# Expert rows by a one-hot product on the tensor engine instead of by table and indirect gather, with three smaller moves, in a two-layer decoder kernel

## The reference, cut to what matters

```
x  += RWKV7(RMSNorm(x));  x += MoE0(RMSNorm(x))
kv  = RMSNorm(x) @ kv_w, compression MLPs
x  += NSA(RMSNorm(x), kv, rel_bias);  x += MoE1(RMSNorm(x));  out = RMSNorm(x)

MoE: group = argmax(xf @ w_gr + b)          (4 groups)
     the 2 best of the group's 8 experts, weights by softmax
     y[t] = sum over its 2 experts e:  weight * (silu(xf[t] @ w1[e]) * (xf[t] @ w3[e])) @ w2[e]
```

## Time and profile before

| | |
|---|---|
| median of 3 runs | 2521.4 us (2521.04 to 2523.46) |
| the profiled execution's own time | 2524.04 us |
| its span | 2521.7 us |
| busy over the span | PE 82%, DVE 29%, ACT 19%, POOL 15% |
| chain that ended last, by engine | PE 60%; DMA 30%; DVE 5%; issue 3%; ACT 2%; POOL 1% |
| of it, the line DMA arena<-m_w (expert weights) | 26% |
| stages (us from the start) | start and projections 0 to 284; bonus loop to 320; scan to 708; w_o to 792; MoE 0 to 1429; NSA to 1886; MoE 1 and the end to 2522 |

### The profile page before, as it was taken

The page is one execution under the profiler, slowest core; times in us unless marked ns, Lnnn a source line. Parts: engine busy times, 40 slices in busy tenths (PEclk is TensorE's granted clock), DMA queues, the critical chain, the costliest instruction groups (busy, mean ns, idle before and its releaser), DMA issues.

```text
span 2521.7 us, 27879 instructions
## 1 busy us (share of the span) xinstructions
PE 2076.5 (82%) x10398; PEld 1168.3 (46%) x10398; DVE 723.1 (29%) x1800; ACT 484.5 (19%) x1207; POOL 372.4 (15%) x650
## 2 busy tenths in 40 slices
PE   8999799999988488778778299988884988877882
PEld 5344289999944233323222147755533333333330
DVE  4204855555574210000000330455403100000002
ACT  2212244444421000000000101255400000000001
POOL 0000366666500100000000100011101000000001
PEclk9999799999998598988899599999995989889996
DMA  9622000000016499999998621100023999999994
GB/s 269 87 75 67 8 2 2 2 2 2 2 51 255 135 400 402 403 402 394 398 403 334 240 67 34 67 26 18 10 100 139 373 401 403 408 405 401 407 417 154
DMA packets 59720, 514.69 MB, mean 204 GB/s; under 512 B 8548, under 2 KB 13412, under 8 KB 42694
## 3 DMA queue, kind: packets, MB, share of 16 engines
q1 hardware_dynamic: 41414, 470.94, 48.7%
q0 software_dynamic: 7936, 25.18, 2.9%
q10 hardware_dynamic: 10240, 16.79, 1.9%
HBM read 475.17 MB, written 36.66 MB: 203 GB/s over the span
## 4 chain that ended last, share of the span: by engine, by line
PE 60%; DMA 30%; DVE 5%; issue 3%; ACT 2%; POOL 1%; SPq 0%; ACTq 0%; DVEq 0%; POOLq 0%; PEldq 0%
PE bank L1269 55%; DMA arena<-m_w 26%; PE bank L1734 2%; DMA arena<-x_rows,ints 1%; DMA arena<-y_rows,ints 1%; PE bank L1279 1%; PE bank L1466 1%; ACT arena L567 1%; POOL token_table L508 1%; DVE arena L1084 0%; DMA y_rows<-arena 0%; PE bank L1541 0%; PE bank L1527 0%; DVE arena L1220 0%; DVE arena L890 0%
## 5 line engine op out<-in xcount | busy, mean ns | idle before, releaser
L1269 PE MATMUL bank<-arena 128*64 128x512 f32 (+10 forms) x8274 | 1805.2, 476 | 213.2 <-DMA arena<-m_w 145.6
L1269 PEld LDWEIGHTS bank<-arena 128*128 128x128 f32 (+3 forms) x8274 | 934.8, 175 | 951.7 <-issue 856.7
L664 ACT ACTIVATE arena<-bank 128x256 f32<-128x256 f32 (+3 forms) x512 | 176.6, 351 | 218.7 <-PE bank L1269 160.8
L692 ACT ACTIVATE arena<-bank 128x512 f32<-128x512 f32 x64 | 38.2, 597 | 900.0 <-PE bank L1269 900.0
L1084 DVE COPY arena<-bank 128x256 f32<-128x256 f32 x64 | 27.1, 424 | 591.0 <-PE bank L1541 591.0
L517 POOL DMA_INDIRECT arena<-x_rows,ints x64 | 57.2, 895 | 880.7 <-PE bank L1527 872.0
L446 POOL TENSOR_TENSOR arena<-arena,const 128x128 f32<-128x128 f32 x384 | 164.6, 458 | 105.2 <-PE bank L1269 83.7
L1068 DVE TENSOR_TENSOR arena<-bank,vec 128x512 f32<-128x512 f32 x64 | 44.3, 692 | 348.2 <-PE bank L1527 348.2
L1527 PE MATMUL bank<-const,arena 64*128 64x64 f32 x512 | 70.3, 280 | 64.8 <-DMA arena<-x_rows,ints 64.8
L1527 PEld LDWEIGHTS bank<-const,arena 64*128 64x128 f32 x512 | 61.3, 200 | 114.2 <-DMA arena<-x_rows,ints 67.2
L788 ACT ACTIVATE arena<-arena,small 128x128 f32<-128x128 f32 (+3 forms) x128 | 70.6, 553 | 96.8 <-DVE small L1220 96.8
(11 more groups left out here) (197 smaller groups left out, 1185.1 us busy)
## 6 DMA issues: line engine op xcount, KB each, us to landing
arena<-m_w SPq DMA_DIRECT2D x64, 4096.0 KB, 36.9
arena<-m_w SPq DMA_DIRECT2D x64, 2048.0 KB, 27.3
y_rows<-arena ACTq DMA_DIRECT2D x128, 128.0 KB, 12.8
y_rows<-arena SPq DMA_DIRECT2D x2, 3840.0 KB, 39.8
arena<-kv_w SPq DMA_DIRECT2D x3, 2048.0 KB, 13.6
rev_bias<-arena SPq DMA_DIRECT2D x1, 5120.0 KB, 69.1
arena<-a_wk SPq DMA_DIRECT2D x8, 512.0 KB, 16.5
arena<-a_wv SPq DMA_DIRECT2D x8, 512.0 KB, 3.5
```

What stands on the lines that cost most here:

```text
L664: nc.scalar.activation(dst(n), src, ACT.Copy).then_inc(sem("ev_" + name), 1)
L1269: return nc.tensor.matmul(dst, lhsT, rhs, start=start, stop=stop)
```

## The change

In the MoE, the normed x, the token table, the index arithmetic for it and the row gathers are gone. DVE makes, for a pair of experts (2p, 2p + 1), a matrix `onehot` of 512 tokens by 128 slots from the place of each token, times the token's 1/rms. PE multiplies columns of `h` with it, which gives the transposed rows of both experts at once: 8 feature blocks of 4 products (128 x 128 with 128 columns), in two halves q. DVE evacuates each half with the gain. `xgT` holds two pairs. The part of the slot arithmetic that serves the results is kept, behind the first pair's work on DVE.

SP's `moe_loads` loses the store of x, the table and the waits for the gathers; the wait of `w_q` moves to `combined` 8 (the end of MoE 0). The bias tables leave the start: their loads are issued after the projections' weights, their 55 products run in groups of 7 in the bonus loop, and ACT evacuates them after it. In NSA, ACT's copy stands ahead of the exponentials in each tick. The path for experts with over 64 tokens is rewritten in the same way and is not shown; no instruction of it is in the trace.

```diff
@@ SP
-            sp.dma_start(fwd, ...); sp.dma_start(rel[0:32, :], ...); sp.dma_start(rev, ...)
             sp.dma_start(h, d["x"]...)
...
-            (the stores of zeros to y_rows, y_clear)
                     if q == 4:
-                        sp.wait_ge(sem("rev_ev"), 1)
-                        sp.dma_start(cmp_dram, bias_made).then_inc(sem("cmp_bias"), 16)
-                        sp.dma_start(rev_dram, spread(rev_rows, 1, P)).then_inc(sem("rev_out"), 16)
+                        sp.wait_ge(sem("zero_rows"), 1)
+                        (the stores of zeros to y_rows, y_clear)
...
+            sp.wait_ge(sem("mix_ready"), 48)
+            (loads of fwd, rel, rev)
+            sp.wait_ge(sem("rev_ev"), 1)
+            sp.dma_start(cmp_dram, bias_made).then_inc(sem("cmp_bias"), 16)
+            sp.dma_start(rev_dram, spread(rev_rows, 1, P)).then_inc(sem("rev_out"), 16)
...
@@ moe_loads
-                    if e == 1:
-                        for j in range(NJ):
-                            sp.wait_ge(sem("xn_ready"), 4 * (1 + 2 * l) + j + 1)
-                            sp.dma_start(x_rows[l][P * j:P * j + P, :], xn_m[:, j, :]).then_inc(sem("x_rows_out"), 16)
-                    if e == 2:
-                        sp.wait_ge(sem("table_out"), 128 * (l + 1))
-                        sp.dma_start(rows_i, table[l]...).then_inc(sem("rows_in"), 16)
-                        sp.wait_ge(sem("gather0"), 16 * (E // 2 * l + 1))
-                        sp.wait_ge(sem("gather1"), 16 * (E // 2 * l + 1))
...
-            sp.wait_ge(sem("hidden_mm"), E)
+            sp.wait_ge(sem("combined"), 8)
             sp.dma_start(w_q, ...)
@@ moe_pool: the 8 table writes and the 32 gathers per layer are removed
@@ ACT, after the loop of operands_act
+            act.wait_ge(sem("bias_mm"), 1)
+            (the four copies L582 to L585, the last with rev_ev)
...
+                        if name == "y" and n == 0:
+                            act.wait_ge(sem("cmp_bias"), 16)
@@ ACT, NSA tick: the block of pT_act (n = tick - 2) stands before the block of Exp (n = tick)
@@ moe_dve, after two_hot
+                dve.wait_ge(sem("place_mm"), at("place_mm", l + 1))
+                then(nc.vector.scalar_tensor_tensor(posm, bank[1][:, 0:128]..., 1.0, two_hot, ALU.add, ALU.mult))
+
+                def one_hot(p):
+                    at_p = onehot[:, p % 2, :, :]
+                    if p >= 2:
+                        dve.wait_ge(sem("gathered_T"), E * l + 2 * p - 2)
+                    then(nc.vector.tensor_tensor(at_p..., spread(spread(cst("iota1"), 1, 2), 1, NJ),
+                                                 spread(posm[:, :, 2 * p:2 * p + 2], 3, CAP), ALU.is_equal))
+                    nc.vector.tensor_tensor(at_p, at_p, spread(rstd, 2, P), ALU.mult).then_inc(sem("onehot_ready"), 1)
+
+                def x_out(p, q):
+                    dve.wait_ge(sem("gathered_T"), E * l + 2 * p + q + 1)
+                    if q == 0 and p >= 2:
+                        dve.wait_ge(sem("hidden_mm"), E * l + 2 * p - 2)
+                    nc.vector.tensor_tensor(xgT[:, p % 2, 4 * q:4 * q + 4, :], bank[2 + q]..., gain, ALU.mult
+                                            ).then_inc(sem("xgT_ready"), 1)
+
+                one_hot(0); x_out(0, 0); x_out(0, 1); one_hot(1)
+                (then the weights of the results, position, count and the slot arithmetic)
...
                     (gated of expert e)
+                    if e % 2 == 0 and e < E - 2:
+                        x_out(e // 2 + 1, 0); x_out(e // 2 + 1, 1)
                     (hT of expert e)
+                    if e % 2 == 1 and e < E - 4:
+                        one_hot(e // 2 + 2)
@@ PE
-            (55 bias products and 2 wide ones, bias_mm, before the first transposes)
...
             for m in range(NP):
                 pe.wait_ge(sem("rk_ready"), m + 1)
-                mm(bank[m][:, :], head_ones, tmp[:, 3, m % 2, :]).then_inc(sem("bonus_mm"), 1)
+                if m >= 4:
+                    pe.wait_ge(sem("bonus_ev"), m - 3)
+                mm(bank[m % 4][:, :], head_ones, tmp[:, 3, m % 2, :]).then_inc(sem("bonus_mm"), 1)
+                if m == 0:
+                    (waits for proj_ev 24, bias_in 48, rel_mask)
+                for at_m in range(7 * m, min(7 * m + 7, NOFF)):
+                    mm(bank[4 + at_m // 32][...], fwd[:, 864 - 16 * at_m:992 - 16 * at_m], rel)
+            mm(bank[6][0:NH, :], rel, rev[:, 0:512])
+            mm(bank[7][0:NH, 0:128], rel, rev[:, 512:640]).then_inc(sem("bias_mm"), 1)
+            pe.wait_ge(sem("rev_ev"), 1)
@@ moe_pe
-                def transpose_rows(n): (8 transposes of xg)
+                def gather(p, q):
+                    pe.wait_ge(sem("onehot_ready"), E // 2 * l + p + 1)
+                    if l or p:
+                        pe.wait_ge(sem("xgT_ready"), E * l + 2 * p + q - 1)
+                    for k in range(4):
+                        for j in range(NJ):
+                            last = mm(bank[2 + q][:, P * k:P * k + P], h[:, j, 4 * q + k::NK], onehot[:, p % 2, j, :],
+                                      j == 0, j == NJ - 1)
+                    last.then_inc(sem("gathered_T"), 1)
...
-                transpose_rows(E * l); transpose_rows(E * l + 1)
+                gather(0, 0); gather(0, 1)
                 first_half(E * l)
                 for e in range(E):
-                    if e < E - 2:
-                        transpose_rows(n + 2)
+                    if e % 2 == 0 and e < E - 2:
+                        gather(e // 2 + 1, 0)
                     if e < E - 1:
                         first_half(n + 1)
+                    if e % 2 == 0 and e < E - 2:
+                        gather(e // 2 + 1, 1)
                     (transpose_gated, result of n)
```

More of the change, by code:

```diff
@@ L231, in decoder_program @@
         row_in, block_of, is_over, slot_f = (scratch(NJ * 2) for _ in range(4))
-        over_cmp = region(2)[:, 0:32 * OVER].rearrange("p (b e) -> p b e", b=OVER)
-        over_expert = region(2)[:, 512:528]
+        posm = scratch(NJ, 32)
+        over_rel = scratch(NJ, 2)
+        over_cmp = region(2)[:, 512:512 + 32 * OVER].rearrange("p (b e) -> p b e", b=OVER)
+        over_expert = region(2)[:, 992:1008]
         over_ids, over_count = ints[:, 120:136], ints[0:1, 136:137]
-        over_rows_i = ints[0:CAP, 137:138]
         combine_w = small[:, 88:96].rearrange("p (j c) -> p j c", c=2)
         slot_i = ints[:, 0:8].rearrange("p (j c) -> p j c", c=2)
[L238 to L242, removed]
         y_rows = [nc.dram_tensor(f"y_rows{l}", (SLOTS, D), FP32, kind="Internal").ap() for l in range(2)]
-        table = [nc.dram_tensor(f"token_table{l}", (SLOTS, 1), I32, kind="Internal").ap() for l in range(2)]
         xT_kv = region(2).rearrange("p (k t) -> p k t", k=NK)
@@ L317, in _ @@
                     if q == 4:
-                        sp.wait_ge(sem("rev_ev"), 1)
-                        sp.dma_start(cmp_dram, bias_made).then_inc(sem("cmp_bias"), 16)
-                        sp.dma_start(rev_dram, spread(rev_rows, 1, P)).then_inc(sem("rev_out"), 16)
+                        sp.wait_ge(sem("zero_rows"), 1)
+                        for l in range(2):
+                            sp.dma_start(y_rows[l][E * CAP:SLOTS, :].rearrange("(p q) c -> p q c", p=OVER * 8),
+                                         spread(zero_rows[0:OVER * 8, :], 1, CAP // 8)).then_inc(sem("y_clear"), 16)
                     if q >= 4:
@@ L780, in _ @@
             for tick in range(len(UNITS) + 4):
+                n = tick - 2
+                if 0 <= n < len(UNITS):
+                    m, b, j = UNITS[n]
+                    act.wait_ge(sem("probs_mm"), at("probs_mm", 2 * n + 2))
+                    if n >= 2:
+                        act.wait_ge(sem("O_mm"), at("O_mm", n - 1))
+                    nc.scalar.activation(probs_T[:, n % 2, 1, 0:P * (j + 1)], bank[5][:, 0:P * (j + 1)],
+                                         ACT.Copy).then_inc(sem("pT_act"), 1)
                 n = tick
@@ L1040, in moe_dve @@
                 then(nc.vector.tensor_copy(over_ids[:, 0:OVER], over_expert[:, 0:OVER]))
-                then(nc.vector.tensor_copy(ints[:, 136:137], over_upto[:, 31:32]))
                 for c, hot in enumerate((hot1, hot2)):
@@ L1273, in norm_transpose @@
                 for k in range(NK):
-                    if i == 0 and k == 4:
-                        pe.wait_ge(sem("rev_ev"), 1)
                     for j in range(NJ):
@@ L1520, in moe_pe, with hidden @@
                 last.then_inc(sem("place_mm"), 1)
-                def transpose_rows(n):
-                    pe.wait_ge(sem(f"gather{n % 2}"), 16 * (n // 2 + 1))
-                    if n >= 2:
-                        pe.wait_ge(sem("xgT_ready"), n - 1)
-                    for k in range(NK):
-                        last = nc.tensor.transpose(bank[2 + n % 2][:, CAP * k:CAP * k + CAP], xg[:, n % 2, k::NK],
```

(14 more changed lines are left out.)

164 lines of the change are left out of this document (66 added, 98 removed).

## The result

The changed kernel takes 2633.4 us (median of 4 runs, 2629.61 to 2635.05), the kernel before 2521.2 beside it (4 runs): ratio 1.0445, 95% interval [1.0429, 1.0462]. It is 112 us slower; the forecast was 107 us faster. The profiled execution has a span of 2633.1 us.

A forecast was written before the change was run, and what follows sets the result against it. It took DMA time, mostly weights, to bound the expert loop, and PE with its waits NSA's loop. Terms -3 - 78 - 8 - 18 = -107 from 2524.0 gave 2417, as a median 2415 us; range 2385 to 2452.

The forecast's parts named there:

- MoE, before the stream: Between the places' end and the first hidden product: 64 new gather instructions at 0.12 to 0.21 us each, 12 us.
- Rival (a): Expert loops: PE takes over as bound, at a mixed 16.9 us per expert, 31 us more, 2445; chance 0.14.
- (e): Expert loops: gathers hold PE at 1.2 GHz, above 3200; slower than before from 18.3 us per expert; chance 0.02.
- t0: Predicted start of MoE 0's first hidden product, 850 us (846 to 854), with 29 expert loads still to go.
- The stream's own rate: Expert loops: without the indirect gathers' 4.5%, weights take 16.44 and 16.28 us per expert; both layers together -78 us.
- (d): All goes well: high clock in bonus loop, 16.0 us per expert, NSA at PE's own time; 2388; chance 0.12.
- (b): Expert loops: the gathers were free to the stream, 17.1 us per expert stay, 44 us more, 2457; chance 0.07.
- Start and bonus loop: Moving the bias work: start gains 14 us, seven loop iterations cost 7 and the end 4; net -3.
- The scan: Scan stage: the new bias table writes to DRAM run there while its DMA is idle, costed at nothing.
- MoE 0's end: Result gathers after MoE 0: with w_q's load behind combined, the first is 7.3 us shorter; -8 us in all.
- NSA: NSA loop: ACT's copy ahead of the exponentials gives -13 us and a higher clock 5 us; -18 in all.
- The gap: Start of each layer's weight stream: DMA idles 9.4 us because expert 3's w2 waits for expert 0's result products.

The follow-up runs named there:

- e5_contig: The changed kernel with features dealt to blocks as 128 neighbours, so that gather products and the transposes before the router read contiguous columns: 2367.7 us, ratio 0.9396 to the kernel before.

## Why the prediction was wrong

**The step that failed** is the price of the gather instruction ("MoE, before the stream"): "None like them is in the trace. Below: 0.11 each, the router's rate at the high clock; above: 1.09 / 8 = 0.136 for a strided load of PE's stationary side". The gather takes 0.244 us an instruction. The upper bound was no bound. L1527 does load 128 columns at a step of 8 floats, and so does `norm_transpose` of the earlier trace rows with all 128 rows; both are transposes, which take 0.11 us from start to start at the high clock with the step or without it (the 0.136 is that plus the end of the last of the eight). What did not carry over is the kind of instruction: from a transpose to a float32 product. The right reading of the rows was that none shows a product with a step, and a price of double was open. Its 32 instructions per expert cost 4 us more than I took, PE's 15.5 us per expert became 19.4, and PE passed the weights' 16.4.

**What it made of the time.** Rival (a), PE takes over the loop, had the mechanism, and I gave it 0.14 with a price of 31 us. It came at the high clock and not the low one, and past (e)'s point of 18.3 us per expert. From the first hidden product (863.4, 13 us later than t0, 10 of them the scan's) to PE's last result (1472.8) MoE 0 takes 609 us. The prediction has 9.4 + 28.67 x 16.44, and as before 22.8 from the last weights to the last result: 503.5. That is 106 us, and 3.6 in the first gathers (15.55 for 12); twice that, for two layers, is 219 of the 222.6 us by which the two MoE stages missed. A PE-bound loop also pays for all 32 experts, where the stream had three in store.

**The stream's own rate** was mis-sized on the other side: 16.4 us per expert, measured 15.4 without gathers. I took the queue's share of engine time for its price. Had the gather instruction cost 0.12 us as I thought, the time would have been about 2368 (run e5_contig), below my range: two errors of opposite sign. The sentence in (d), "if the store and gather neighbours slowed the weights", was right for the gathers. Two sums of the rivals are off by 2 us, without effect on the range: (b) is 2415 + 44 = 2459 and (d) 2415 - 37 = 2378.

**Start and bonus loop**: the terms held. The k-projection's first result came 12.7 us earlier (14 predicted), the loop took 5.10 us per iteration and +7.6 (+7), the end +4.2 (+4). The clock was as the earlier trace rows said. In the window of the bonus loop after,

```profile
274.00:323.00 49.00, 45.55 (x142) 31.08 (x142) 30.99 (x45) 10.18 (x25) 29.58 (x23) 0.50 0.06 14
```

PE is 93% busy and the clock is 0.50 on average. The Trainium skill (TensorE: Matmul & The Clock Gate, Part 1: The HAM clock gate) says that activity releases the throttle; here it did not.

**The scan**: "The new writes of the bias tables to DRAM run in the scan, whose DMA is idle", costed at nothing. I asked who shares the data queue and not who else could be held up. +11.

**MoE 0's end**: the result gather takes 5.64 us against 12.73, and the stretch from the last result to the norm is 6.6 shorter (8 predicted).

```profile
1486.85 5.64 DMA arena<-y_rows,ints
```

**NSA**: right in sign, mis-sized: -18 predicted, -33 in the loop. PE's idle time fell from 28 to 12 us, 16 and not 13, and the clock rose from 0.92 to 1.00, so that its busy time fell from 159 to 142, 17 us where I took 5. At 0.92 PE loses 8% of 187 us, 15: the term was in the earlier trace rows, and I gave back a third of it. The order of ACT's copy does this alone: in the kernel with only that change the same window's clock is 1.00 and PE works 141 of 154 us.

**The gap** of 9.4 us at the stream's start is not in the time: swapping the queue's order changed nothing. In a loop that PE binds the stream makes it up.

## What to carry to other kernels

Before PE reads an operand with a step, find a row with that step in the same kind of instruction: here the transposes with the step were cheap and the float32 products were not. Without such a row, price the product at contiguous and at double, and lay data out so that the columns are neighbours. When a change puts work on the engine that is second in line, work out how near it comes (here 15.5 against 16.4) and ask what one mis-sized term would do: that sets the chance of the rival. A queue's share of the DMA engines need not be all that it costs its neighbours (here 0.77 against 1.8 us per expert). And a long store into a stretch whose DMA is idle was not free.

## What the runs showed of the hardware

- Float32 products of 128 x 128 with 128 columns, per instruction at the high clock: 0.12 us with steps of 1 and 2 floats between the columns of the stationary operand, 0.24 with 4 and 8, and 0.24 with step 8 on the moving side; with 64 moving columns and step 8 still 0.24. The strided product took 0.240 us at a granted clock of 0.50 too, where the contiguous one took 0.213.
- Float32 transposes of 128 x 128 at the high clock: 0.11 us each with step 8 and with step 1.
- An indirect gather of 64 rows of 4 KB for every 6 MiB of a weight stream of 368 GB/s (110.27 MB in 300 us) took 4.5% of the DMA engines' time and lengthened the stream by 12% (15.4 to 17.2 us per 6 MiB).
- Under a store of 5 MB, 54 us long, PE stopped twice (2.5 and 3.2 us) with no wait shown and its clock fell; the stage ended 8 to 15 us later than with the store cut into 8.
- In a bonus loop filled with bias products the granted clock was 0.50 over 49 us with PE 93% busy; in the expert loop with gathers among the hidden and result products it was 0.99 to 1.00.
